# A two-layer hybrid decoder step on one core: four experts of 32 slots on four column groups of TensorE, routing, experts and combine in one phase, and column groups in the decode attentions

## What is computed

```python
# decode latent attention: 8 sequences x 1024 cached rows of 128, 4 heads
# memory attention: 8 decode tokens x 256 memory rows, 4 heads
e_glob = g_idx * EXPERTS_PER_GROUP + e_idx          # top group of 4, then top 2 of its 8 experts
comb = einsum('mk,mke->me', e_w, one_hot(e_glob, 32))
act = silu(einsum('md,edf->mef', xf, w_gate)) * einsum('md,edf->mef', xf, w_up)   # d=1024, f=256
y = einsum('mef,efd->md', act * comb[:, :, None], w_down)
```

## Time and profile before

| | |
|---|---|
| three runs | 1689.72, 1697.03, 1700.62 us (median 1697.03) |
| the profiled execution | 1686.48 us, its span 1684.6 us |
| mean granted TensorE clock | 0.943 of full |
| layer 2: routing, experts, combine | 33.8, 249.1, 16.6 us |

### The profile page before, as it was taken

The page is one execution under the profiler, slowest core; times in us unless marked ns, Lnnn a source line. Parts: engine busy times, 40 slices in busy tenths (PEclk is TensorE's granted clock), DMA queues, the critical chain, the costliest instruction groups (busy, mean ns, idle before and its releaser), DMA issues. The chain is left out here.

```text
span 1684.6 us, 22437 instructions
## 1 busy us (share of the span) xinstructions
PE 1491.5 (89%) x7812; PEld 980.9 (58%) x7812; DVE 747.8 (44%) x1544; ACT 387.4 (23%) x832; POOL 39.4 (2%) x46
## 2 busy tenths in 40 slices
PE   6988988969887899999889889789698878999997
PEld 3967577956566533333559675679465665333335
DVE  4675536473453322222446645373734533222224
ACT  1124313100212322222111243121003123222221
POOL 0040000000000000000001300000000000000000
PEclk9998999969999899999989989999699988999999
DMA  4461021125132899999135500212252338999991
GB/s 181 150 205 46 0 61 56 62 78 225 59 122 94 329 377 391 388 394 407 56 121 171 187 32 0 66 51 83 68 213 81 111 113 327 383 382 392 387 391 73
DMA packets 62313, 307.91 MB, mean 183 GB/s; under 512 B 13296, under 2 KB 16128, under 8 KB 35968
## 3 DMA queue, kind: packets, MB, share of 16 engines
q1 hardware_dynamic: 59136, 296.10, 46.1%
q0 software_dynamic: 3072, 10.49, 1.9%
HBM read 352.91 MB, written 3.98 MB: 212 GB/s over the span
## 5 line engine op out<-in xcount | busy, mean ns | idle before, releaser
L2230 PE MATMUL bank<-m_w,moe_hb 128*64 128x512 f32 x1280 | 287.1, 601 | 0.0
L509 PE MATMUL bank<-hT,wf 128*128 128x264 f32 x1024 | 251.0, 404 | 33.0 <-PEq L216 20.3
L509 PEld LDWEIGHTS bank<-hT,wf 128*128 128x128 f32 x1024 | 201.2, 200 | 75.3 <-issue 23.9
L2230 PEld LDWEIGHTS bank<-m_w,moe_hb 128*64 128x64 f32 x1280 | 89.1, 138 | 163.4 <-issue 162.7
L2328 DVE SCALAR_TENSOR_TENSOR tm<-bank,moe_scale,tm 128x256 f32<-128x256 f32 x40 | 19.4, 484 | 299.9 <-ACT tm L2300 299.9
L2347 DVE COPY m_YS<-bank 128x256 f32 x160 | 64.2, 422 | 51.7 <-issue 37.8
L2300 ACT ACTIVATE tm<-bank,moe_scale 128x256 f32<-128x256 f32 x40 | 19.0, 474 | 270.7 <-PE bank L2230 270.7
L2264 PE MATMUL bank<-m_w,tm 128*64 128x512 f32 x320 | 73.1, 598 | 0.9 <-ACT tm L2313 0.9
L2264 PE MATMUL bank<-moe_w,moe_aT 128*64 128x512 f32 x320 | 73.1, 598 | 0.0
L1784 PE MATMUL bank<-brT,wbr 128*128 128x264 f32 x256 | 60.7, 397 | 11.6 <-DMA wbr<-in_w_br 7.6
L288 PE MATMUL bank<-proj_hsp,proj_wsp 128*128 128x264 f32 x224 | 64.5, 288 | 1.9 <-DVE proj_wsp L282 1.9
(11 more groups left out here) (544 smaller groups left out, 2179.7 us busy)
## 6 DMA issues: line engine op xcount, KB each, us to landing
m_w<-in_w_x SPq DMA_DIRECT2D x200, 1024.0 KB, 10.5
moe_w<-in_w_x SPq DMA_DIRECT2D x40, 1024.0 KB, 7.0
wf<-in_w_gate SPq DMA_DIRECT2D x64, 512.0 KB, 3.6
proj_wfm<-in_w_fm SPq DMA_DIRECT2D x28, 512.0 KB, 4.3
wbr<-in_w_br SPq DMA_DIRECT2D x16, 512.0 KB, 3.6
mix_wo<-in_w_out SPq DMA_DIRECT2D x16, 512.0 KB, 4.1
mem_wkv<-in_w_kv SPq DMA_DIRECT2D x2, 2048.0 KB, 8.0
mem_ckT<-in_memkT SPq DMA_DIRECT2D x2, 2048.0 KB
```

The costliest lines, as they stand in the source:

```text
L509: mm = pe.matmul(E["bank"][to][:, 0:T], F["wf"][slot][:, k, :], E["hT"][:, k, :], start=k == 0, stop=k == KT - 1)
L2230: mm = pe.matmul(bank[s][W * g:W * g + W, :], hb[s][:, 4 * i + k, W * g:W * g + W], ring[s][i][g][:, COLS * k:COLS * k + COLS], start=i == ...
```

## The change

- **Window 32, quads.** W = 32 and four experts are worked at once on four column groups. `ORDER` is b0 b1 b2 s0 b3 s1 b4 s2 b5 s3 b6 b7: 8 base quads and 4 spill quads (16 spill places), 12 in all. A quad has 6 pieces, (v,0) to (v,3) gate and up, (v,4) and (v,5) down; each piece is four loads of 128x1024 (512 KB), one per expert.
- **Ring.** Seven slots of one piece. The first seven base pieces go to all; later base pieces use five, spill pieces two. `plan()` sorts the loads by the use that frees their slot, and SP issues them in that order. Every load of a spill piece reads its two registers afresh.
- **One phase.** Routing, experts and combine are one phase `moe`; the ring is loaded from its start.
- **Gather per two quads.** `gather(p, k)`: 5 matmuls 128x256 for each of 8 blocks, between the matmuls of the quad before; `slot_scales` 12 tiny ones.
- **Combine per quad.** `down` writes slots on the partitions, so `turn_out`, HS, YS and the combine phase go. ScalarE copies the high part, VectorE takes the low, `combine(v, d)` is 2 matmuls 128x264 per block, added to xT by VectorE (`add`), eight per quad.
- **Decode.** In `mlad` the two halves of the scores go to two column groups side by side, all before the transposes; the 64 matmuls over the cache alternate between two groups (banks 5 and 6), and VectorE copies and adds the second. In `memory` scores and outputs go the same way.

```diff
-W = 64
+W = 32
+RING, SPILL_RING = 7, 2
+def plan():
+    home, loads, last, uses = {}, [], {}, {}
+    seen = {"base": 0, "spill": 0}
+    for at, (v, j) in enumerate(PIECES):
+        kind = ORDER[v][0]
+        n = seen[kind]
+        seen[kind] += 1
+        if kind == "spill":
+            slot = RING - SPILL_RING + n % SPILL_RING
+        else:
+            slot = n if n < RING else (n - RING) % (RING - SPILL_RING)
...
+        loads.append((last.get(slot, 0), at, v, j, slot))
+        last[slot] = at + 1
+    return home, [(v, j, slot, release) for release, at, v, j, slot in sorted(loads)]
...
             for i in range(16):
-                mm = pe.matmul(bank[5][0:32, 0:MEM], qblk[:, i, :], ckT[:, i // 2, i % 2, :], start=i == 0,
-                               stop=i == 15)
+                g = i % 2
+                mm = pe.matmul(bank[5 - 3 * g][32 * g:32 * g + 32, 0:MEM], qblk[:, i, :], ckT[:, i // 2, g, :],
+                               start=i < 2, stop=i >= 14)
...
-            for half in range(2):
-                for n in range(N):
+            for n in range(N):
+                for half in range(2):
                     at = PAGES * n + 4 * half
-                    mm = pe.matmul(bank[half][0:32, :], qblk[:, n, :],
+                    mm = pe.matmul(bank[half][32 * half:32 * half + 32, :], qblk[:, n, :],
...
+            pe.wait_ge(S("own_copied"), 1)
...
-                    mm = pe.matmul(bank[5][0:32, 0:RANK], pblk[:, p, n, :], ck[:, n, RANK * p:RANK * p + RANK], start=i == 0,
-                                   stop=i == NPG - 1)
+                    i, g = N * p + n, n % 2
+                    mm = pe.matmul(bank[5 + g][32 * g:32 * g + 32, 0:RANK], pblk[:, p, n, :],
+                                   ck[:, n, RANK * p:RANK * p + RANK], start=i < 2, stop=i >= NPG - 2)
...
+            for v, j, slot, release in LOADS:
+                kind, b = ORDER[v]
+                i, at = j // 2, slice(HALF * (j % 2), HALF * (j % 2) + HALF)
+                if release:
+                    sp.wait_ge(S("piece_done"), release)
...
+                for g in range(4):
+                    if kind == "base":
+                        sp.dma_start(ring[slot][g][:], A["w_x"][l, 4 * b + g, i][:, at]).then_inc(S(f"w{slot}_loaded"), 16)
+                    else:
+                        k = 4 * b + g
+                        e = sp.value_load(items[0:1, k:k + 1], min_val=0, max_val=NE - 1)
+                        used = sp.value_load(items[0:1, SPILL + k:SPILL + k + 1], min_val=0, max_val=1)
+                        sp.dma_start(ring[slot][g][:], A["w_x"][l, e, i][:, at], cond=used)\
+                            .then_inc(S(f"w{slot}_loaded"), 16)
...
+                for k in (2 * j, 2 * j + 1):
+                    for g in range(4):
+                        mm = pe.matmul(bank[s][W * g:W * g + W, :], hb[p % 2][:, k, P * s + W * g:P * s + W * g + W],
+                                       w[g][:, COLS * (k % 2):COLS * (k % 2) + COLS], start=k == 0, stop=k == KT - 1)
+                mm.then_inc(S("piece_done"), 1)
...
+            for v in range(N):
+                p = v // 2 + 1 if v % 2 == 0 and v + 2 < N else 0
+                for j in range(4):
+                    if v + 1 < N:
+                        gate_up(v + 1, j)
+                    for x in (2 * j, 2 * j + 1):
+                        if v:
+                            combine(v - 1, x)
+                        if p:
+                            gather(p, x)
+                    if j == 1:
+                        turn(v)
+                down(v, 0)
+                if p:
+                    slot_scales(p)
+                down(v, 1)
```

More of the change, by code:

```diff
@@ new lines, in moe, with done, base_slot @@
+        aT = [spare[:, 512:768].rearrange("p (f w) -> p f w", f=2), ph.sb("aT1", [P, 2, P])[:]]
+        high = ph.sb("high", [P, D_MODEL], F32R)
+        low = ph.sb("low", [P, D_MODEL], F32R)
+        ring = [[ph.sb(f"w{s}{g}", [P, HALF]) for g in range(4)] for s in range(RING)]
+        LG, CNT, SLOT, XROW = 5, 6, 7, 1
+        PARTS = ((0, 0), (2, 0), (1, 1), (3, 1), (4, 2))
+        def done(v, j):
+            return PIECES.index((v, j)) + 1
+        def base_slot(v):
+            kind, b = ORDER[v]
+            return b + (0 if kind == "base" else NE // 4)
@@ new lines, in _ @@
+            for k in range(KT):
+                gather(0, k)
+            slot_scales(0)
+            gate_up(0, 0)
+            for c, (t0, n) in enumerate(CHUNKS):
+                mm = pe.transpose(bank[LG][0:2, t0:t0 + n], tok[0:n, :, c], ident[0:n, 0:n])
+            mm.then_inc(S("tokT_done"), 1)
+            pe.matmul(bank[CNT][0:NE, 4:5], C("stri")[0:NE, 0:NE], ncnt[:, 1:2], start=True, stop=True)\
+                .then_inc(S("off_done"), 1)
+            gate_up(0, 1)
+            pe.wait_ge(S("tokT_ready"), 1)
@@ L2025, in _ @@
+            for d in range(KT):
+                combine(N - 1, d)
         @ph.b.scalar
@@ L2351, in _ @@
+                step(vec.tensor_copy(rows[:, r, :], bank[5 - r][:, 0:T]), wait=r == 1)
+            dve.wait_ge(S("items_done"), 1)
+            for r in range(2):
+                step(vec.tensor_copy(items[:, SPILL * r:SPILL * r + SPILL],
+                                     bank[CNT][0:1, 32 + SPILL * r:32 + SPILL * r + SPILL]), "items_ready", wait=False)
             product(0)
             for v in range(N):
+                if v:
+                    for d in range(KT):
+                        add(v - 1, d)
@@ L2432, in moe @@
[L2432 to L2445 removed]
+                if v % 2 and v + 3 < N:
+                    one_hots((v + 3) // 2)
@@ L2448 @@
+                places(v)
+                if v % 2 == 0 and v + 2 < N:
+                    slot_scales(v // 2 + 1)
+                for h in range(2):
+                    cs = slice(COLS * h, COLS * h + COLS)
+                    dve.wait_ge(S("high_ready"), 2 * v + h + 1)
+                    low_part(nc.vector, low[:, cs], bank[4 + h][:], high[:, cs]).then_inc(S("low_ready"), 1)
+            for d in range(KT):
+                add(N - 1, d)
 PHASES = [layer]
```

719 lines of the change are left out of this document (284 added, 435 removed).

## The result

The changed kernel takes 1785.12 us (median of four runs, 1781.92 to 1787.19) beside 1694.36 for the kernel before: 1.053 times as long, with a 95% interval of 1.049 to 1.057. The forecast was 1706 and its range ended at 1765. The direction and the place were right, the size was not.

The account below looks back on a forecast made before the run. SP's issue of loads was taken to bound the experts: +43 us in two layers, decode -34, net +9 on the profiled 1686.5, so 1695.5; the median 10.5 above, 1706. Range 1628 to 1765; the forecast's own 1690 to 1722.

Parts of the forecast that it names:

- What bounds the changed kernel: Expert phase: SP's issue of loads, 50.3 us per couple of quads against TensorE's 36.8 and the DMA's 30.6; +21.5 per layer.
- A base piece costs SP 2.1 us: Expert phase, SP's queue: four loads at 0.53 us each, so six base pieces take 12.6 us.
- the three cycles: Expert phase: couples of six base and six skipped spill pieces, 12.6 + 37.7 = 50.3 us each on SP.
- the four pieces of s0: Expert phase: SP never waits after (s0,2) and issues four skipped spill pieces of s0 in 25.1 us, to 113.4.
- the start: Routing and first experts: 16 base pieces at the DMA's pace, 81.6 us; SP gets to (s0,2) at 88.3.
- the last stretch: End of experts: nine base pieces 46.4 us, landing 2.0, last down 1.8, tail about 6.5; end at 321.0.
- My bounds for this part: Experts: 6.6 us per skipped spill piece, +6.6 per layer; DMA at 4.9 or 5.3 us, -5 or +5 per layer.
- Waits and sizes on TensorE: TensorE in the experts: a piece 1.73 us, four groups abreast; a couple of quads 36.8 us with waits.
- Decode -34 us: Both decode attentions: latent -12.0 us and memory -5.0 us, so -17.0 per layer, -34 in all.
- Rival A: Experts: SP is not the bound, a spill piece costs about 2 us; -39 us, median 1624; chance 0.18.
- rival C: TensorE in the experts: four groups run in twos, a couple takes 57.4 us; median 1818; chance 0.09.
- Rival B: Experts: the clock falls where TensorE waits; some +11 us per layer, median 1728; chance 0.21.

## Why the prediction was wrong, step by step

- **What bounds the changed kernel: right.** SP's fixed order, with six skipped spill pieces of four loads; 36.4 us measured where 37.7 were forecast, the TENSOR_LOAD at 0.27 us, and three holes in the DMA's work. The figure of about 600 ns for a `tensor_load` floor, from the Trainium skill ("DMA: Bandwidth & Descriptors", Latency and other measured facts), isn't borne out here: its estimate would have put a spill load at 2.2 us, the trace has 1.5.
- **A base piece costs SP 2.1 us: this step failed.** The 0.53 us per load came from ten loads at the start of routing, when the queue was empty, and I used it for a queue kept full. The change doubles the packets for the same bytes. A stretch of 24 base loads took 20.5 to 21.6 us instead of 12.6, so a piece cost SP 3.4 to 3.6 us, because its issues stall when the queue is full of packets. Of the 44 us a layer that were missed (365 for 321), some 25 are the three cycles, 8 to 9 us each (59.0 for 50.3); the four pieces of s0 gave 1 back. About 14 are the start, where the spill loads of (s0,2) came 102 us into the phase and not 88. The windows of that stretch and of the phase's last 13 us:

```profile
1409.90:1463.50 53.60, 38.06 (x261) 21.61 (x265) 19.70 (x77) 12.20 (x26) 0.50 (x2) 0.78 0.99 386
1475.00:1512.00 37.00, 25.02 (x154) 9.15 (x153) 10.01 (x20) 3.35 (x7) 0.00 (x0) 0.82 0.98 380
1762.00:1775.30 13.30, 9.47 (x52) 4.87 (x52) 6.47 (x15) 1.07 (x2) 0.00 (x0) 0.76 0.01 4
```

In the start the DMA was busy all the time, at 384 GB/s from 1409.9 to 1512, where 5.1 us a piece had meant 411: some 5 of the 14 us are this rate (16 pieces at 5.46). The rest fits the stall, since SP could not pass the 21st piece until all but about 4.8 MB had moved (21 pieces are 44.0 MB, and 39.2 went in the 102 us). The last 6 us are the last stretch, 62.8 us for 56.7: the transfers ended 2 to 3 us late, and what follows them took over 13 us where 10.3 were added up; there the clock (0.76) may have a share, which no run separates.

The kernel with 16 KB rows, in which no issue stalls, comes to (s0,2) after 89 us, has cycles of 50.7 and 52.8 and ends after about 326. That is near the forecast's numbers, in part by luck: its DMA moved 420 GB/s up to (s0,2), faster than forecast, and its cycle is closed by TensorE's releases and not by SP's issues. My bounds for this part (1.65 us per skipped load, DMA at 5.3 us a piece) didn't include the stall, since no row of before showed one.

- **Waits and sizes on TensorE: right.** Four groups abreast; a piece 1.92 us with the tail for 1.73; a couple of quads 37.1 us for 36.8, once TensorE is what bounds it.
- **Decode -34 us: right.** 36 measured. Its parts shifted: the cache matmuls take 8.8 us two abreast, not 7.7.
- **Rival A (SP not the bound)** fell with the reads once per quad, **rival C (only two abreast)** with the piece's 1.92 us. **Rival B (the clock)** had the sign right and the mechanism wrong: the granted clock did fall, to 0.82 over the phase, but in the cycles it cost the changed kernel nothing, because SP had the end and waited for no engine. The rule on short bursts between waits for a DMA, from the Trainium skill ("TensorE: Matmul & The Clock Gate", HAM oscillation), describes what the rows show (3.64 us for a piece behind a wait of 10 us); that it makes the time is not so here. Filling the wait was worth at most some 9 us, and only after the reads were gone.
- **The chances.** The chance of slower by over 1% was 0.42, and all of it sat on B and C or just above the bound. None sat on a higher price for the base loads, a term of the step that the forecast itself called decisive.

## What to carry to other kernels

When the bytes of a load are halved, count the packets in flight, not only the issues: this queue took loads every 0.5 us while it had room and then at 0.9 us and more, and everything behind in its fixed order waits. Loads that mostly do nothing (conditional ones, with registers to read) belong on a queue of their own, their registers read once and ahead of the wait; here that turned 5% slower into 4% faster (0.959, where the decode part alone gives 0.977), and rows of 16 KB made it 5%. And price a queue by its rows under the load that the change will put on it.

## What was unexpected in the hardware

An issue on SP's queue took 0.33 us for 14 loads of 128 packets and then mostly 0.9 to 3.1 us each, with some 1,100 to 1,300 packets of 4 KB still ahead (about 5 MB), while 14.7 MB in packets of 16 KB went in without a stall. Packets of 4 KB moved at 409 GB/s and of 16 KB at 426 to 427 by the pages' slices of the two kernels without spill quads, worth 19 us where the DMA was the bound. A skipped conditional DMA cost about 0.4 us on SP and GpSimd alike, and its two register reads over a microsecond.
